# Two LRU halves that count on a semaphore each, a later head sum, and identities ahead of the scaled rows

## The reference

```python
p = x @ w_in[l]
y_rwkv = rwkv7_time_mix(token_shift(p[..., :RWKV_COLS], ...), ...)   # delta-rule state, 6 heads
y_lru = rglru_mix(p[..., RWKV_COLS:RWKV_COLS + LRU_COLS], ...)       # 4 blocks of 64
y_sba = stick_breaking_attention(p[..., RWKV_COLS + LRU_COLS:], ...) # 6 heads
x = layer_norm(ALPHA * x + concat(y_rwkv, y_lru, y_sba) @ w_out[l])
x = layer_norm(ALPHA * x + grouped_moe(x))
```

```python
xc = conv(xin, conv_w) + conv_b                     # causal, 4 wide
gate_a = sigmoid(xb @ wa + ba); gate_x = sigmoid(xb @ wx + bx)
log_a = -LRU_C * gate_a * softplus(-lam); a = exp(log_a)
b_in = sqrt(-expm1(2 * log_a)) * (gate_x * xc)
h = scan(a, b_in)                                   # h_t = a_t h_(t-1) + b_t
y = head_rms_norm(gelu(gate_in) * h, norm_g, LRU_BLOCKS)
```

## Time and profile before

| | |
|---|---|
| median of 3 runs | 1338.48 us (1337.44 to 1338.96) |
| the profiled execution | 1337.05 us |
| its span | 1335.3 us |
| PE busy | 1226.3 us (92%) |
| DVE busy | 514.3 us (39%) |
| ACT busy | 382.4 us (29%) |
| POOL busy | 163.5 us (12%) |

### The profile page before, as it was taken

How to read it: one execution, slowest core, us unless ns; L and a number is a source line. 1 busy time by engine, 2 the same in 40 slices (tenths; PEclk the granted TensorE clock), 3 DMA queues, 4 the chain that set the end, 5 groups by cost and what they waited for, 6 DMA issues and landing times.

```text
span 1335.3 us, 23315 instructions
## 1 busy us (share of the span) xinstructions
PE 1226.3 (92%) x9686; PEld 594.8 (45%) x9686; DVE 514.3 (39%) x879; ACT 382.4 (29%) x575; POOL 163.5 (12%) x230
## 2 busy tenths in 40 slices
PE   8998799999989999998999956999999999999980
PEld 3443344444567777775445532333333333333320
DVE  7265522344258777774364353111111111111117
ACT  1043312234145555555222112111111111111114
POOL 4141010000022221210000001010101010101010
PEclk9999899999989999999999977999999999999995
DMA  5100001010000000001704009785889499397126
GB/s 221 48 32 31 32 31 48 32 32 16 0 2 3 35 3 35 3 3 65 268 8 158 27 34 360 283 287 184 283 321 308 154 311 374 91 371 253 50 41 257
DMA packets 61013, 170.18 MB, mean 127 GB/s; under 512 B 3184, under 2 KB 3312, under 8 KB 60928
## 3 DMA queue, kind: packets, MB, share of 16 engines
q1 hardware_dynamic: 54384, 145.31, 28.9%
q0 software_dynamic: 6544, 23.63, 7.3%
HBM read 144.29 MB, written 24.64 MB: 127 GB/s over the span
## 4 chain that ended last, share of the span: by engine, by line
PE 84%; DVE 7%; ACT 4%; DMA 3%; issue 2%; SPq 0%; POOL 0%; POOLq 0%; DVEq 0%; ACTq 0%
PE PS L1967 32%; PE PS L341 9%; PE PS L1438 8%; PE PS L240 8%; PE PS L350 3%; PE PS L797 3%; PE PS L1132 2%; PE PS L816 2%; PE PS L1141 2%; PE PS L1151 2%; PE PS L1960 2%; PE PS L486 1%; PE PS L1578 1%; PE PS L872 1%; DMA XS<-in_xT 1%
## 5 line engine op out<-in xcount | busy, mean ns | idle before, releaser
L1967 PE MATMUL PS<-XS,YT 128*64 128x512 f32 x656 | 286.2, 593 | 2.1 <-DMA SQ<-in_w_upx 1.2
L1967 PE MATMUL PS<-SQ,YT 128*64 128x512 f32 x488 | 214.7, 593 | 0.0
L1967 PE MATMUL PS<-RK,YT 128*64 128x512 f32 x672 | 211.1, 593 | 0.0
L1967 PEld LDWEIGHTS PS<-XS,YT 128*64 128x64 f32 x656 | 88.5, 137 | 183.3 <-issue 180.1
L341 PE MATMUL PS<-XS 128*128 128x512 f32 x288 | 129.5, 607 | 6.4 <-DMA XS<-in_xT 6.1
L2055 DVE TENSOR_TENSOR YT<-YT,PS 128x256 f32<-128x256 f32 x42 | 15.8, 418 | 271.7 <-PE PS L1967 271.7
L1438 PE MATMUL PS<-SQ,YT 128*128 128x512 f32 x256 | 114.0, 594 | 0.6 <-issue 0.6
L1967 PEld LDWEIGHTS PS<-RK,YT 128*64 128x64 f32 x672 | 65.9, 137 | 74.8 <-issue 74.8
L341 PEld LDWEIGHTS PS<-XS 128*128 128x128 f32 x288 | 54.5, 193 | 79.8 <-issue 71.3
L1955 POOL DMA_INDIRECT sums<-YT,RK x21 | 33.6, 1600 | 323.3 <-DVE YT L2068 323.3
L1438 PEld LDWEIGHTS PS<-SQ,YT 128*128 128x128 f32 x256 | 47.7, 190 | 56.7 <-issue 56.5
(11 more groups left out here) (410 smaller groups left out, 1870.7 us busy)
## 6 DMA issues: line engine op xcount, KB each, us to landing
RK<-in_w_down SPq DMA_DIRECT2D x6, 2048.0 KB
XS<-in_w_in SPq DMA_DIRECT2D x21, 512.0 KB, 3.2
XS<-in_w_gate SPq DMA_DIRECT2D x5, 2048.0 KB
XS<-in_w_upx SPq DMA_DIRECT2D x5, 2048.0 KB
XS<-in_w_down SPq DMA_DIRECT2D x5, 2048.0 KB
RK<-in_w_gate SPq DMA_DIRECT2D x5, 2048.0 KB
SQ<-in_w_gate SPq DMA_DIRECT2D x4, 2048.0 KB
RK<-in_w_upx SPq DMA_DIRECT2D x4, 2048.0 KB
```

What stands on the lines that cost most here:

```text
L1967: ins = e.matmul(acc[r, :], rows[:, r], third_cols(n, k, at, HB), start=start, stop=stop)
```

## The change

There are three edits. **The counts:** `s_ld` becomes a list of two semaphores, one for each half, and every wait on it names the half and the step within the half. `rw_act` waits for both. **The tables:** they are written out. On DVE at n = 6 the convolution of half 1 now stands ahead of L437 of half 0. The last part of half 1 moves from n = 9 to n = 10 on PE, ACT and DVE alike. The rest stays where it was. **The identities:** in block 0 POOL writes them ahead of the scaled rows and keys, in later blocks where it did before.

```diff
         s_mp, s_me, s_md = sem("quarter_products_in_psum"), sem("quarters_copied_act"), sem("quarters_added_dve")
-        s_ld, s_la, s_lp = sem("lru_dve"), sem("lru_act"), sem("lru_pe")
+        s_ld = [sem(f"lru{u}_dve") for u in range(2)]
+        s_la, s_lp = sem("lru_act"), sem("lru_pe")
...
         def lru_dve(e, u):
             A, B, Cc, Dd, G, X = lru_bufs(u)
-            n = [u * LD]
+            n = [0]
 
             def step(ins):
-                ins.then_inc(s_ld, 1)
+                ins.then_inc(s_ld[u], 1)
                 n[0] += 1
                 return n[0]
 
             def own():
-                wait(e, s_ld, n[0])
+                wait(e, s_ld[u], n[0])
...
                 e.activation(B, G, ACT.Square).then_inc(s_la, 1)
-                wait(e, s_ld, u * LD + 6)
...
                     wait(e, s_const, CONSTS)
-                    wait(e, s_ld, u * LD + 4)
+                    wait(e, s_ld[u], 4)
                     wait(e, s_la, (u - 1) * LA + 11 if u else 0)
...
                 if g == 0:
-                    wait(e, s_ld, 2 * LD)
+                    for u in range(2):
+                        wait(e, s_ld[u], LD)
...
         def mats_pool(e):
+            def identities(b):
+                wait(e, s_pm, NM1 * b)
+                wait(e, s_pw, b)
+                eye = ident2[:, :].rearrange("p (o c) -> p o c", o=1).broadcast_to([P, NH, C])
+                for x in (T_, U_):
+                    ins = e.tensor_copy(x.rearrange("p (n c) -> p n c", n=NH), eye)
+                ins.then_inc(s_init, 1)
             for b in range(NB):
                 tk, _ = tile_of(b)
                 wait(e, s_rd, RD * NPAIR)
                 if b == 0:
                     wait(e, s_pp, CT + NT)
+                    identities(0)
                 wait(e, s_pk, 3 * b)
                 dec = pc[:, :, 2 * b:2 * b + 2].rearrange("p g (c o) -> p g c o", o=1).broadcast_to([P, NPAIR, 2, C])
...
@@ -762,12 +772,8 @@
                 e.tensor_copy(KS[DIAG[1], 1, :], KB[DIAG[1], 1, tk]).then_inc(s_mo, 1)
                 wait(e, s_mo, b + 1)
 
-                wait(e, s_pm, NM1 * b)
-                wait(e, s_pw, b)
-                eye = ident2[:, :].rearrange("p (o c) -> p o c", o=1).broadcast_to([P, NH, C])
-                for x in (T_, U_):
-                    ins = e.tensor_copy(x.rearrange("p (n c) -> p n c", n=NH), eye)
-                ins.then_inc(s_init, 1)
+                if b > 0:
+                    identities(b)
...
-        LRU_AT = [LRU_T + 3 * u for u in range(2)]
         RW_AT = [RW_END + 2 * g for g in range(NPAIR)]
-        PE_AFTER, ACT_AFTER, LRU_DVE_AFTER = {}, {RW_END - 1: [(rw_pre_act,)]}, {}
-        for u, n in enumerate(LRU_AT):
-            PE_AFTER[n] = [(lru_pe, u, 0), (lru_pe, u, 1)]
-            PE_AFTER[n + 2] = [(lru_pe, u, 2)]
-            for part in range(3):
-                ACT_AFTER[n + part] = [(lru_act, u, part)]
-                LRU_DVE_AFTER[n + part] = u
+        PE_AFTER = {4: [(lru_pe, 0, 0), (lru_pe, 0, 1)], 6: [(lru_pe, 0, 2)], 7: [(lru_pe, 1, 0), (lru_pe, 1, 1)],
+                    10: [(lru_pe, 1, 2)]}
+        ACT_AFTER = {4: [(lru_act, 0, 0)], 5: [(lru_act, 0, 1)], 6: [(lru_act, 0, 2)], 7: [(lru_act, 1, 0)],
+                     8: [(lru_act, 1, 1)], 10: [(lru_act, 1, 2)], RW_END - 1: [(rw_pre_act,)]}
+        LRU_DVE_AFTER = {4: (0, 0), 5: (0,), 6: (1, 0), 7: (1,), 8: (1,), 10: (1,)}
...
@@ -2198,12 +2201,8 @@
             lru = [lru_dve(e, u) for u in range(2)]
 
             def after(n):
-                if n == LRU_AT[0]:
-                    next(lru[0])
-                if n in LRU_DVE_AFTER:
-                    next(lru[LRU_DVE_AFTER[n]], None)
-                if n == LRU_AT[0] + 2:
-                    next(lru[1])
+                for u in LRU_DVE_AFTER.get(n, ()):
+                    next(lru[u], None)
```

More of the change, by code:

```diff
@@ L445, in lru_act @@
                 e.activation(B, G, ACT.Square).then_inc(s_la, 1)
-                wait(e, s_ld, u * LD + 6)
+                wait(e, s_ld[u], 6)
                 wait(e, s_la, u * LA + 1)
@@ L454, in lru_act @@
                 e.activation(Dd, PS[3][:, :], ACT.Sigmoid, bias=v1(V_BX + u)).then_inc(s_la, 1)
-                wait(e, s_ld, u * LD + 7)
+                wait(e, s_ld[u], 7)
                 wait(e, s_masksd, 1)
@@ L470, in lru_act @@
             e.activation(Cc, Cc, ACT.Exp, scale=v1(V_NC + u)).then_inc(s_la, 1)
-            wait(e, s_ld, u * LD + 9)
+            wait(e, s_ld[u], 9)
             wait(e, s_la, u * LA + 6)
@@ L475, in lru_act @@
             e.activation(X, B, ACT.Ln, scale=2.0).then_inc(s_la, 1)
-            wait(e, s_ld, u * LD + 10)
+            wait(e, s_ld[u], 10)
             wait(e, s_la, u * LA + 8)
             e.activation(A, A, ACT.Exp, scale=0.5).then_inc(s_la, 1)
-            wait(e, s_ld, u * LD + 13)
+            wait(e, s_ld[u], 13)
             wait(e, s_la, u * LA + 9)
```

## The result

The changed kernel takes 1324.82 us, the median of 4 runs (1321.77 to 1325.38), beside 1338.72 us for the kernel before. The ratio is 0.9892, with a 95% interval from 0.9876 to 0.9907: 1.1% faster. On the 1338.48 us that the prediction started from, the ratio makes 1324.0 us, just under the low end of its range. It was forecast 10.5 us faster and came out 14 to 14.5 us faster. The profiled execution took 1321.77 us and is the quickest of the four. Its span, against the 1335.3 of before, is 15.3 us shorter.

A forecast was written before the change was run, and what follows sets the result against it. TensorE (PE) was taken to bound the kernel, its waits before the last matmul paid in full. Gains of 4.9 + 3.85 + 1.75 = 10.5 us gave a forecast of 1328.0 us, range 1324.4 to 1332.2.

The forecast's parts named there:

- Part 1: Gate matmuls, n=6: convolution moved ahead cuts PE's wait from 4.2 to 1.0 us and saves 1.7 of clock: 4.9 us.
- Part 2: Second sum over heads, n=9 to n=10: the 9.2 us wait becomes 5.3 in front of P5: 3.85 us gained.
- I charge 1.65 again: Product P5 of n=8: half clock after the new 5.3 us wait costs 1.65 us.
- Part 3: Start of block 0: identities first on POOL shorten PE's wait of 3.16 us: 1.75 us gained.
- the low bound: Block 0: POOL's copies, now running beside DVE, stretch, so part 3 gains 0.9 us less.
- I take 1.75 without it: Block 0: part 3 counted at 1.75 us, without any gain from the clock staying up.
- rival A: Clock stays up after the new wait, in block 0, or both: 1326.3 us with one, 1324.9 with both; chance 0.22.
- The upper bound of 2.7 us: Block 0: if the shorter gap leaves the clock up, some 2.7 us of half-clock time could go.
- B: New wait longer than thought, DVE chain stretched by POOL's sums: 4.3 us less gain, 1332.3 us; chance 0.12 with unmoved convolution.
- the unmoved convolution: DVE at n=6: the convolution doesn't move at all, leaving 1332.9 us; its chance is counted within B's 0.12.
- D: No change: the lead is absorbed by a wait for something not released by PE, 1338.5 us; chance 0.03.
- C: Slower: clock stays low long after the new wait; 30 us more at half clock gives 1343.0 us; chance 0.03.

The follow-up runs named there:

- the first trace: The profiled execution of the changed kernel, quickest of its four runs: 1321.77 us.
- kernel 6: The kernel before, with the two semaphores and 13 idle matmuls filling PE's 3.16 us gap at the start of block 0: ratio 0.9982, block 0 32.54 us.

## Why the prediction was right or wrong

**Part 1 was right.** The order on DVE, the stretched L403 (1.75 us), the remaining wait (0.83 forecast as 1.0) and the gate matmuls at full clock came out as worked out: 4.21 - 0.83 = 3.4 us of wait and 1.7 of clock. Where the price of half clock behind that wait is concerned, 1.7 was one value of two: other traces of that wait have 2.7 and 2.8.

**Part 2: the mechanism was right, one term was mis-sized.** The new wait is at P5 of n=8, put down to the add, and 5.34 us long, where 5.3 was forecast. The step that failed is "I charge 1.65 again". Six traces with this wait unfilled show 3.1, 2.8, 2.9, 1.9, 1.5 and 1.5 us, 2.3 in the mean, and in the first trace part 2 gave 7.46 - 5.08 = 2.4 us where 3.85 was forecast. I took the size from two waits in one trace, as if it belonged to the wait. It lasts as long as the clock stays at 0.50 after the restart: the mean granted clock up to the next product is 0.54 to 0.56 where the price was 3.1, 2.9 and 2.8, 0.66 where it was 1.9, and 0.70 and 0.71 where it was 1.5.

**Part 3: the wait was right, the rest of the block was not.** The gap shrank by 1.67 us where 1.75 was forecast, both engines meeting as worked out, and the low bound fell away. The Trainium skill says in SBUF — State Buffer, section Who interferes with whom, that a DVE instruction with at most one input from SBUF, outside the modes that use two ports, does not contend with GpSimd. The trace agrees: POOL's two copies of L768 took 0.52 us beside DVE's L1001, as they did before without it, and L1001 took 1.81 us where it had taken 1.82. The one long L758 of before (1.45 us for two, at 487.58) ran beside a scan on DVE (L1205, 486.98 to 488.71), as the prediction supposed. The step that failed is "I take 1.75 without it", with rival A's value of 1.5. The block at full clock is not 1.5 but 4.1 us shorter than in the trace of before (kernel 6), and the changed kernel had it so in both of its traces. **This is what put the time below the forecast:** without these 4 us the median would lie near the forecast. The trace could have said more. The upper bound of 2.7 us came from the stretch that was seen at 0.50, but there was a second fall further in, behind a wait of 1.65 us, that the bound left out:

```profile
384.00:387.00 3.00, 3.00 (x55) 2.53 (x51) 2.53 (x5) 0.64 (x2) 0.00 (x0) 0.50 0.02 5
```

And the waits on ACT that I let eat half of the gain did not grow when PE got faster: they come to 2.2 us over block 0 in both traces, since ACT's copies are released by PE and came earlier with it.

**The sum.** 7.46 (parts 1 and 2) + 1.68 (the gap) + 4.06 (block 0's clock) + 1.6 (the last block's clock) + 0.5 (the start) = 15.3 us in the first trace. The waits alone give 3.4 + 3.9 + 1.7 = 9.0 us, which is 8.9 in the forecast's own numbers (3.2 + 3.9 + 1.75). The forecast charged as much clock as it credited in part 2 and left it out elsewhere. The error of 4.8 us in this trace is block 0's clock (4.1), the last block's (1.6) and the start (0.5), less the 1.5 too little charged in part 2. The last block's share and the start are chance, and this trace is the quickest of four: the median's surplus is 3.5 to 4 us. A slip in the working had no part in it: the range is said to end with B, yet 1332.9, the unmoved convolution that is counted with B, lies outside it.

**The rivals.** A came half true: the clock stayed up in block 0, and not behind the new wait. It had a chance of 0.22, which was too little, and a price that was too low (1.5 us for block 0, 4.1 measured). B and D did not happen; the chain on DVE ran as before, and the lead reached the end. C did not happen either. In no trace did the half clock behind the new wait outlast the first product, and a clock stuck low for more than 50 us, which the Trainium skill notes in TensorE: Matmul & The Clock Gate, section Seeing it yourself, is not shown by any run here.

**What stays open.** The single moves together give 17 us (ratios 0.9942, 0.9966 and 0.9964) against 14.5 for all at once; each ratio is known to 1.4 to 2.3 us, so the difference is not shown to be real. What they give beyond their waits is clock in stages that I have not taken apart run by run. Whether block 0 keeps the clock in every execution of the changed kernel is not known either: there are two traces of it. Why block 0 at 359.6 and 360.0 keeps the clock and at 362.0 doesn't was not settled, only that something beside the gap has a part in it, the moment or what PE did ahead of the block.

## What to carry to other kernels

When a move shortens a wait of PE, the time that comes back has two terms: the wait, which can be read off to a tenth of a microsecond, and the half clock behind it, which spread here from nothing to 4 us and belongs to the sum and to the range. Fill the gap with idle matmuls in one run to measure the second term by itself before blaming the order of the work. And when PE's wait has moved to another place, look at what is queued in front of the instruction that releases it: here moving a chain of five DVE steps behind the adds gave some 6 us on top of the 14 of the whole change.

## What the runs showed of the hardware that was not expected

The same wait, of the same length and at the same place in the program, is followed by half-clock work of different cost: 1.5 to 3.1 us behind the 5.3 us wait (six traces), 1.7 to 2.8 us behind the wait of 4.0 to 4.2 us (five traces). The granted clock, 0.54 to 0.71 up to the next product, says that the difference is the time at half clock left after the restart. The clock also falls amid thin work without a long gap: in block 0, with no gap over 1.65 us, five traces of seven lost 1.5 to 2.9 us. Small bf16 matmuls in the gap were enough to keep the granted clock at 1.00 through the block in both kernels that had them.
